# A two-block network on one core: norms of block 2 folded into the layers, and the stick-breaking chain's table asked for ahead of its wait

## The reference, cut to what matters

```python
def second_block(x, c, norm_g, w_ada, b_ada, w_in, sinks, w_br_a, ..., w_out, final_g):
    h = x
    for l in range(DEPTH):                      # 2 layers
        h = hybrid_layer(h, ...)
    return rms_norm_2(h, final_g)

def hybrid_layer(x, c_silu, ...):
    shift, scale, gate = split(c_silu @ w_ada + b_ada, 3)
    u = rms_norm_2(x, norm_g) * (1 + scale) + shift
    z = u @ w_in                                # queries, keys, values, gates of three branches
    ya = dsa_attention(...)      # indexer scores, top 128 of the keys, softmax
    yb = swa_sinks_attention(...)
    yc = stick_breaking_attention(...)          # 8 heads, log-sigmoids and a running sum
    merged = sigmoid(ma) * (ya @ w_br_a) + sigmoid(mb) * (yb @ w_br_b) + sigmoid(mc) * (yc @ w_br_c)
    return x + gate * (merged @ w_out)

def stick_breaking_attention(q, k, v):
    z = q @ k.T * dh ** -0.5
    log_beta, log_1m = log_sigmoid(z), where(s < t, log_sigmoid(-z), 0)
    after = reversed_cumsum(log_1m) - log_1m
    return where(s < t, exp(log_beta + after), 0) @ v
```

## Time and profile before

| | us |
|---|---|
| median of 3 runs (3738.13 to 3740.82) | 3740.18 |
| the profiled execution, its own time | 3740.58 |
| its span, first to last instruction | 3738.8 |
| PE busy in the span | 3441.9 (92%) |
| DVE busy | 1735.3 (46%) |
| ACT busy | 1082.2 (29%) |

### The profile page before, as it was taken

The page is one execution under the profiler, slowest core; times in us unless marked ns, Lnnn a source line. Parts: engine busy times, 40 slices in busy tenths (PEclk is TensorE's granted clock), DMA queues, the critical chain, the costliest instruction groups (busy, mean ns, idle before and its releaser), DMA issues. The chain is left out here.

```text
span 3738.8 us, 41780 instructions
## 1 busy us (share of the span) xinstructions
PE 3441.9 (92%) x16316; PEld 2294.5 (61%) x16316; DVE 1735.3 (46%) x2986; ACT 1082.2 (29%) x1678; POOL 38.6 (1%) x42
## 2 busy tenths in 40 slices
PE   7999997999988999996999987999999989999998
PEld 5766673444455866673444445777766767767666
DVE  7766633212236866633212134457644344666443
ACT  4343321101124334322101023353333124433321
POOL 1000000000000100000000000000000000000000
PEclk9999997999998999997999998999999999999999
DMA  5521128999944431127999952212311231222122
GB/s 190 192 88 57 58 93 339 423 424 424 423 176 153 182 104 57 57 85 297 423 424 424 423 228 86 69 62 65 94 68 68 102 110 47 73 67 85 68 85 95
DMA packets 129183, 653.28 MB, mean 175 GB/s; under 512 B 21972, under 2 KB 32212, under 8 KB 61944
## 3 DMA queue, kind: packets, MB, share of 16 engines
q1 hardware_dynamic: 129016, 650.98, 45.0%
HBM read 632.54 MB, written 14.72 MB: 173 GB/s over the span
## 5 line engine op out<-in xcount | busy, mean ns | idle before, releaser
L1629 PE MATMUL ps<-normed_T_hi,ring_split 128*128 128x512 f32 (+1 forms) x1952 | 627.9, 403 | 20.1 <-PEq L264 14.8
L1629 PEld LDWEIGHTS ps<-normed_T_hi,ring_split 128*128 128x128 f32 (+1 forms) x1952 | 365.6, 191 | 123.5 <-issue 42.1
L1629 PE MATMUL ps<-normed_T_lo,ring_split 128*128 128x512 f32 (+1 forms) x976 | 385.6, 395 | 0.0
L2278 PE MATMUL ps<-normed_T_hi,ring_split 128*128 128x512 f32 x1024 | 336.0, 410 | 8.9 <-DVE branches L2544 7.6
L1906 DVE TENSOR_TENSOR ring_split<-weight_ring,ring_split 128x2048 fp32r<-128x2048 f32 x76 | 174.0, 2289 | 169.9 <-ACT ring_split L1790 169.6
L2278 PEld LDWEIGHTS ps<-normed_T_hi,ring_split 128*128 128x128 f32 x1024 | 192.7, 191 | 81.8 <-issue 32.7
L1629 PEld LDWEIGHTS ps<-normed_T_lo,ring_split 128*128 128x128 f32 (+1 forms) x976 | 185.6, 190 | 41.6
L2278 PE MATMUL ps<-normed_T_lo,ring_split 128*128 128x512 f32 x512 | 202.6, 396 | 0.0
L1685 PE MATMUL ps<-branches 128*128 128x512 f32 x384 | 173.0, 593 | 3.3 <-issue 3.0
L1230 PE MATMUL ps<-weight_ring,projected 128*64 128x512 f32 x768 | 167.9, 593 | 0.0
L1790 ACT ACTIVATE ring_split<-weight_ring 128x2048 fp32r<-128x2048 f32 x76 | 144.7, 1909 | 61.5 <-DMA weight_ring<-in_w_slabs 53.2
(11 more groups left out here) (422 smaller groups left out, 5996.6 us busy)
## 6 DMA issues: line engine op xcount, KB each, us to landing
weight_ring<-in_w_slabs SPq DMA_DIRECT2D x78, 1024.0 KB, 4.9
weight_ring<-in_w_exp_gate SPq DMA_DIRECT2D x48, 1024.0 KB, 16.1
weight_ring<-in_w_exp_down SPq DMA_DIRECT2D x48, 1024.0 KB, 12.1
weight_ring<-in_w_exp_up SPq DMA_DIRECT2D x48, 1024.0 KB, 19.8
weight_ring<-in_w_branch_gate SPq DMA_DIRECT2D x32, 1024.0 KB, 4.8
spare_weights<-in_w_exp_up SPq DMA_DIRECT2D x32, 1024.0 KB, 20.8
spare_weights<-in_w_exp_gate SPq DMA_DIRECT2D x32, 1024.0 KB, 20.1
spare_weights<-in_w_exp_down SPq DMA_DIRECT2D x32, 1024.0 KB, 15.5
```

The source lines that it names most:

```text
L1629: ins = e.matmul(dst, lhs(k, m), rhs(k, m), start=k == 0 and m == 0, stop=k == KD - 1 and m == 2)
L2278: ins = e.matmul(dst, lhs(k, m), rhs(k, m), start=k == 0 and m == 0, stop=k == KD - 1 and m == 2)
```

## The change

For block 2 the norm between the layers and the last norm are no longer stages. What is done instead:

1. The last 8 output steps run tile by tile (i = 8, 9 finish tile 0, then tile 1, 2, 3) in PSUM banks 7, 1, 6, 0. Slab 38 is now needed from i = 9 on, not from i = 12; its split is placed at i = 6.
2. As each tile is finished, ACT squares it, DVE makes the variance, ACT the root, DVE the reciprocal and the scaled tile. In layer 0, PE transposes tiles 0, 1 and 2 behind steps 11, 13 and 15; ACT takes the turned first half (tiles 0, 1) out of PSUM in 128x256 pieces, twice for even `k` (once in float32, once rounded to `T_hi`), DVE splits k = 0..3. SP saves tiles 0 to 2, loads slabs 0 and 1 of the next layer, and slab 0 is split by ACT and DVE there.
3. Layer 1 starts with half steps (256 of the 512 tokens, 24 matmuls each): step 0 on the first half, then the transposes of tile 3, step 1 on the first half, then both on the second half, while ACT and DVE finish tile 3 and the second half.
4. At the end of layer 1, DVE writes the final product tile by tile (the last tile in two halves) and SP stores each at once.
5. In the stick chain ACT asks for the table set `natural_log_exp_and_others` before it waits for the logits; Abs reads PSUM directly; the copy out of PSUM is done by DVE (`copy_logits`, in `front`), which first evicts the last step's result.

```diff
+        def turn_tile(e, s, t, n, await_pair):          # PE, 8 transposes
+            e.wait_ge(s["scaled_by_vector"], n)
+            for k in range(KD):
+                if k % 2 == 0 and t % 2 == 0:
+                    await_pair(k // 2)
+                ins = e.transpose(turned_cols(t)(k), U2[:, t, k * P:(k + 1) * P], ident)
+            ins.then_inc(s["turned"], 1)
+        def take_turned(e, s, half, n, ks, again):      # ACT
+            e.wait_ge(s["turned"], n)
+            for k in ks:
+                if again and k >= 4:
+                    e.wait_ge(s["lo_ready"], k - 3)
+                ...
+                e.activation(turned2[:, k, :], src, ACT.Identity, **affine).then_inc(s["turned_taken_scalar"], 1)
+                if k % 2 == 0:
+                    e.activation(T_hi[:, k, half * 256:half * 256 + 256], src, ACT.Identity, **affine).then_inc(s["stage_d"], 1)
...
             for i in range(16):
-                if i % 4 == 0:
-                    weights("out")
+                c, kh, t = (0, i // 4, i % 4) if i < 8 else (1, i % 2, i // 2 - 4)
...
-            starts = {i: q for q, i in first_of.items()}
+            starts = {first_of[q]: q + 1 for q in range(slabs - 2)}
+            starts[out_at[6]] = slabs - 1
...
+                    if turned_by_last:                  # SP, start of layer 1
+                        e.dma_start(x_saved[3 * P:4 * P, :], X[:, 3, :]).then_inc(s["stored"], 16)
+                        e.dma_start(ring_land[:, 2, :], a["w_slabs_2"][l, 2, :, :]).then_inc(slot_loaded[2], 16)
+                        e.wait_ge(s["stored"], 16)
...
+                    if turned_by_last:                  # PE, start of layer 1
+                        half_step(0, 0)
+                        turn_tile(e, s, 3, 1, None)
+                        half_step(1, 0)
+                        half_step(0, 1)
+                        half_step(1, 1)
...
+                    if turned_by_last:                  # ACT, start of layer 1
+                        square(3, slice(512, D))
+                        tile_root(e, s, 3, 1)
+                        take_turned(e, s, 1, 1, range(KD), True)
...
+                    if turned_by_last:                  # DVE, start of layer 1
+                        split_taken(e, s, 0, range(4, KD), False, st_)
+                        last_variance(e, s, 1)
+                        tile_rstd(e, s, 3, 1)
+                        e.tensor_scalar(U2[:, 3, :], X[:, 3, :], rstd2[:, 3:4], None, ALU.mult).then_inc(s["scaled_by_vector"], 1)
+                        split_taken(e, s, 1, range(KD), True, st_)
+                        e.wait_ge(s["stored"], 16)
...
                     def front(h):                       # ACT
-                        e.wait_ge(s["stick_logits"], h + 1)
+                        e.preload_act_table_set("natural_log_exp_and_others")
                         v = ln[:, h % 2, :]
                         if h >= 2:
                             e.wait_ge(s["stick_sums"], h - 1)
-                            e.wait_ge(s["stick_output"], h - 1)
-                        z = wt[:, h % 2, :]
-                        e.activation(z, z_ps, ACT.Copy).then_inc(s["stick_copied"], 1)
-                        e.wait_ge(s["stick_copied"], h + 1)
-                        e.activation(v, z, ACT.Abs).then_inc(s["scalar_step"], st_.add("scalar_step"))
-                        e.wait_ge(s[st_.name], st_.value)
+                        e.wait_ge(s["stick_logits"], h + 1)
+                        e.activation(v, z_ps, ACT.Abs).then_inc(stick_read, 1)
+                        e.wait_ge(stick_read, h + 1)
...
+                    def copy_logits(h):                 # DVE
+                        if h >= 2:
+                            e.wait_ge(s["stick_output"], h - 1)
+                        e.wait_ge(stick_read, h + 1)
+                        e.tensor_copy(wt[:, h % 2, :], z_ps).then_inc(s["stick_copied"], 1)
...
+                        elif what == "front":
+                            evict(last)
+                            copy_logits(n)
...
-        row_norm_stage("g_final", False)
+        row_norm_stage("g_final")
+        norm_stage([(modulation_cols, modulation_saved[0, :, :])], scale_col2, shift_col, save=True, slabs=...)
         for l in range(DEPTH):
-            norm_stage([(modulation_cols, modulation_saved[l, :, :])], scale_col2, shift_col, save=True, slabs=...)
-            layer2_stage(l)
-        row_norm_stage("final_g_2", True)
+            layer2_stage(l, l > 0)
```

More of the change, by code:

```diff
@@ L1897, in _ @@
                             attend(n)
+                    e.preload_act_table(ACT.Sqrt)
+                    for t in range(2):
+                        e.wait_ge(tile_done, t + 1)
+                        square(t)
+                        tile_root(e, s, t, earlier + t + 1)
+                        if t == 0 and next_layer is not None:
+                            e.wait_ge(slot_loaded[0], 16)
+                            e.activation(ring_hi[:, 0, :], ring_land[:, 0, :], ACT.Copy).then_inc(s["slab_hi"], 1)
+                    square(3, slice(0, 512))
+                    if next_layer is not None:
+                        e.wait_ge(columns_loaded, 16)
+                        take_turned(e, s, 0, 2, range(4), False)
+                    e.wait_ge(tile_done, 3)
+                    e.wait_ge(s["var_ready"], earlier + 3)
+                    square(2)
+                    tile_root(e, s, 2, earlier + 4)
+                    if next_layer is not None:
+                        take_turned(e, s, 0, 2, range(4, KD), False)
+                        e.wait_ge(s["turned_taken_scalar"], KD)
+                        e.wait_ge(s["stage_d"], KD // 2)
+                    else:
+                        e.wait_ge(tile_done, 4)
+                        square(3, slice(512, D))
+                        tile_root(e, s, 3, earlier + 5)
                 @block.vector
@@ L1915, in dense @@
                     def dense(i):
[L1916 to L1917 removed]
+                        if i in starts:
+                            to_lo(starts[i])
                         evict(i - 1)
@@ L2096, in _ @@
                             pick(n)
-                    dense(len(steps))
-                    e.wait_ge(s[st_.name], st_.value)
+                    evict(out_at[15])
+                    e.wait_ge(tile_done, NT)
+                    if next_layer is None:
+                        last_variance(e, s, earlier + 5)
+                        scale_tile(3, earlier + 4)
         late_branch = (1, 3, 0, 2)
```

150 lines of the change are left out of this document (130 added, 20 removed).

## The result

The changed kernel takes **3682.12 us** (3679.27 to 3684.51, 4 runs), against 3740.5 for the kernel before on the same chip: ratio 0.9845, 95% interval 0.9828 to 0.9862, so 52 to 64 us less. The gain was 58.4 us in the first set and 53.8 in the second, where 45.5 stood in the sum. The three places of the gain came as forecast; the slow clock, at the boundary and in the stick chain, did not.

What follows compares the result with a forecast made beforehand. PE, busy 92% of the span, was taken as the bound, losing time only where it stands still or runs below its clock. Gains of 12.5 + 8.8 + 24.2 = 45.5 us gave 3694.7 us, range 3684 to 3713.

Steps and rivals of the forecast that it cites:

- (a): Stick chain: the early table load does not last, so the chain gains nothing; 3719 us, chance 0.14 (whole or part).
- (b): Boundary between layers gives back half through half clock and longer ACT pieces: 6 instead of 12.5 us; 3701, chance 0.09.
- (c): Stick chain: DVE's new wait in `front` becomes the bound, making the kernel slower; 3762 us, chance 0.03.
- (d): All three places: everything warm and all 3.6 us of slow clock back, 16 + 10 + 30; 3684 us, chance 0.05.
- Part 1: Boundary between the layers: step 2 of layer 1 starts earlier, worth 12.5 us (8 to 16).
- 12 pieces on ACT, one behind the other, 6.7 us: Boundary: after tile 3 is turned, ACT takes its 128x256 pieces at 0.56 us each, until 3023.2.
- So I take off 1.2: Boundary: pauses ahead of PE's half steps may lower its clock, so 13.7 us gained was cut to 12.5.
- Part 2: End of layer 1: final norm done tile by tile, span ends at 3730.0, worth 8.8 us (7.5 to 10).
- Part 3: Stick chain: log ready 2.5 us earlier in every head, 12.1 us a layer, 24.2 in all (14 to 30).
- I count half of these 1.8: Stick chain, head 3: its 20 matmuls took 6.30 us against head 1's 4.50; 0.9 us a layer counted.
- Head 7: Stick chain: `sums(7)` starts at about 2573.1 against 2577.87, PE waiting 2.2 us; 4.8 us gained a layer.
- DVE is the bound: Stick chain, head 7: DVE works without a pause from Ln of head 6 to `subtract(6)`, which starts 3.1 us earlier.

Runs made afterwards that it cites:

- first set: Changed kernel timed beside the kernel before on the same chip: 3682.12 us against 3740.5, ratio 0.9845.
- the second: Changed kernel and the kernel before timed again on another chip: 3683.76 us against 3737.54, ratio 0.9859.
- full_start: Changed kernel, but layer 1 starts with whole steps in place of half steps, after tile 3 is turned: 3686.13 us, ratio 0.9874.
- last_norm_as_before: Changed kernel with the final norm as a stage of its own again: 3689.78 us.
- round_behind_log: Changed kernel with one DVE sorting round moved from before head 7's logarithm step to behind it, in both layers: 3684.31 us.
- stick_as_before: Changed kernel with the old stick chain (copy, Abs, Exp, table, Ln on ACT): 3710.84 us, and 3709.66 when timed once more.
- before_delayed: Kernel before with 8 more products of 0.21 us ahead of the first step of i >= 3 of every layer: 3738.98 us, ratio 1.0007.
- stick_before_delayed: Changed kernel with the old stick chain and 8 more products ahead of the first step of i >= 3 of every layer: 3713.53 us.

## Why the prediction was wrong

**What bounds the kernel** was read rightly: PE's pauses and its slow stretches. All three parts gained, and the loads left the chain. Rivals (a), (b) and (c) did not come. Rival (d), "everything warm" and 3684, came nearest in time; its clock was not right, since slow stretches are left (head 7 in layer 0, head 1 in layer 1), but two of its three sizes were (16 and 30, against 17.1 and 30.3).

**Part 1 failed, by the same amount in every run.** 17.1 us against 12.5. Four terms, all on one side, make 4.8, and the misread start of step 2 takes 0.2 back.

(1) "12 pieces on ACT, one behind the other, 6.7 us": 5.6 (2996.78 to 3002.37). I took 0.56 a piece, which is right as its length; its pace is 0.45 to 0.47. The Trainium skill's page "ScalarE: Activation LUTs" ("What ACT_TABLE_LOAD costs") says that ACTIVATEs one behind the other overlap by some 93 ns, and this trace agrees, with 0.10 to 0.16; I had only used that page for its drain. The prediction had this as its upper bound ("pieces that overlap"), and the row of the 16 pieces of 777 ns in the earlier trace rows already shows it: their busy time is 11.8 and not 12.4.

(2) "So I take off 1.2" for half clock: not needed, the clock was 1.00, here and in the 13 other traces with half steps. In full_start, where PE stood still for 4.5 us, it fell (0.68 over 16 us); the 0.2 to 1.1 us that are left between the half steps brought it down in no trace.

(3) The half steps were to start 3.6 us behind the last output product (3011.7 - 3008.1) and started at 2.2, since ACT's last six pieces (k = 4..7 of tiles 0 and 1) were over 1.4 us sooner, and some 1.0 of that is again their pace (6 pieces in 2.8 to 2.9 us, twice, where 3.4 each was counted). Tile 3's chain and turn gave 0.3 more.

(4) Two turns cost 1.8 together and not 2.6.

Sum 1.1 + 1.2 + 1.4 + 0.3 + 0.8 = 4.8, of which the pace of the pieces is 2.1 and the reserve for the clock 1.2. Each was a careful choice taken by itself; all err to one side, and together they went beyond the term's own upper bound of 16.

**Part 2 was right**, 8.7 against 8.8, and 8.7 in last_norm_as_before (9.8 in the five traces with the shorter tail).

**Part 3: the waits right, the clock mis-sized.** 30.3 us in the profiled pair against 24.2. The lowest interval that any run shows with the old chain, and with the new: head 0 30.3 and 27.4, head 2 24.90 and 23.35, head 3 24.62 and 22.16, head 6 29.1 and 26.6, head 7 22.9 and 20.6 (the old chain's lowest there still has slow clock in it, as the prediction's term had). Sum 2.9 + 1.55 + 2.46 + 2.5 + 2.3 = 11.7 a layer; the prediction's terms without head 3's 0.9 were 11.2. Above these lowest values the trace of before has 1.5 at head 0, 1.6 at head 1, 1.7 at head 3 and 0.3 at head 7; that of after has 1.7 at head 7 in layer 0, or 1.6 at head 1 in layer 1. The difference is 3.4, where I had counted 0.9: 11.7 + 3.4 = 15.1.

The failed step is "I count half of these 1.8", and with it head 0, whose slow stretch was not looked for. But this term has no fixed size: which slow stretches come differs between layers and runs, in both kernels. By medians the chain is worth 25.9 to 29.3, so this miss is 2 to 5 us, and 6.1 in the profiled pair. Nor does slow clock always cost time: in before, PEclk over head 7's `logits` and the step behind it was 0.62 in layer 0 and 0.74 in layer 1, yet the intervals are 23.2 and 23.1, since `sums(7)` then waited for DVE not at all or 1.46 us. What is slow ahead of a wait is paid out of the wait.

**Head 7** went by its own steps: a wait of 2.2 at `sums(7)`, forecast 2.2; 5.0 us gained over heads 6 and 7 in layer 1, forecast 4.8, and 3.4 in layer 0, where the sums were slow. "DVE is the bound" holds by round_behind_log: with one round moved away the wait went, and came back at the weighing.

**The sum.** Forecast 45.5; with 4.6 more at the boundary, 6.1 in the chain, 1.8 at places that the change does not touch (1.1 + 1.0 - 0.3) and 0.1 less at the end: 57.9. Rival (d), the nearest case, had been given a chance of 0.05. That the time fell just outside the range and not just inside is luck: 1.9 us are less than what separates runs of one kernel. That the sum was low by 8 to 13 us is not.

What stays open: the rule by which a wait of 1.5 to 2.6 us is followed by half clock or not. That the same chance decides the 3 to 10 us between runs of one kernel is likely, as in most kernels the longest run is listed with a lower granted clock than the shortest (3714.57 at 0.967 and 3709.07 at 0.970 in stick_as_before), but only one run of each was traced.

## What to carry to other kernels

A table load can be hidden by asking for it ahead of a wait that ACT has anyway. It gives back time only where an engine waits for the chain behind it, and only up to the length of that wait. Next to a boundary between stages, work on the part of the data that is ready fills the pause and keeps TensorE's clock as well. When you sum small costs, use the pace of a row of equal instructions and not the length of one, and do not add a reserve at each step: keep it for the range.

## What the hardware showed

A wait of 2.3 us was followed by a slow stretch (6.30 us for 20 matmuls) or by none (4.60) with the same code, and one of 1.55 likewise, within one execution. Each costs 1.5 to 1.7 us where nothing behind it waits, and one shift of everything by 1.7 us made it change its place (before_delayed), another did not (stick_before_delayed, heads 2 and 3). The Trainium skill's page "TensorE: Matmul & The Clock Gate" ("What's actually happening") says that the gate does not start its observation with the kernel, so that the same kernel sees its clock change at different instructions; these traces agree. ACT_TABLE_LOAD took 1283 ns in all 16 heads, in before with 0.3 us of idle ahead of it in sum, and in head 3 there Ln started 0.02 us behind its end (2458.15 + 1.28, then 2459.45).
